# Third branch of a merged layer: projection multiplied chunk by chunk into four banks, gates after it

## The chip, the cores and the metric

One core of one Trainium2 chip runs one program. The metric is the device time of one execution in microseconds, as the median of several runs. Everything is float32; products are made of two fp32r parts per operand (below).

## The reference, cut to what matters

The program computes two model blocks on 256 tokens (held as two tiles of 128) of width 1024. The change lies in the first block. Its layer has three branches, whose outputs are projected, gated and summed, and then goes through an output projection and a mixture of 32 experts:

```python
merged = (jax.nn.sigmoid(ga) * (o_a @ w_branch_a)      # o_a: 256 x 1024
          + jax.nn.sigmoid(gb) * (o_b @ w_branch_b)    # o_b: 256 x 1024
          + jax.nn.sigmoid(gc) * (o_c @ w_branch_c))   # o_c: 256 x 2048, the third branch
x = x + gt1 * (merged @ w_out)
h2 = rmsnorm(x, norm2_g) * (1.0 + sc2) + sh2
x = x + gt2 * hier_moe(h2, rg_w, rg_b, re_w, re_b, e_gate, e_up, e_down)
```

`ga`, `gb` and `gc` are columns of `h @ w_in`. Each expert has three matrices of 1024 x 512, so the experts' weights are 32 x 3 x 2 MB = 192 MB, and all of them are read.

## The kernel before, in words

Every engine runs its own list of instructions in order, and they meet only in semaphores. Weights come in loads of 1 MB, issued by SyncE (`fetch`) into a ring of five places named "raw". A load is cut into pieces of 128x1024 elements, two per load. ScalarE copies a piece to a rounded high part H (line 1597), VectorE subtracts it to get the low part L (line 2304), and TensorE multiplies with both: `three` (lines 651 to 653) issues high x high, high x low and low x high. There are four places for H and L, so ScalarE and VectorE run up to three pieces ahead of the one in use (`reach`, `ahead`), and a piece's H waits until TensorE has used the piece four before it. Where an engine's list has an evaluation between two pieces, it stands behind the H or L of up to three pieces further on.

A piece of `gemm2` is 24 matmuls of 128x256. The branch stages run `for i in range(4)`: two pieces of the gate `{name}g{i}` into one bank, then the projection `{name}w{i}`. For the third branch (name "C") the projection has depth 2048, so it takes four pieces and two banks. ScalarE makes the sigmoid of the gate, VectorE multiplies it with the projection (line 2560), GpSimd adds the product to the merged sum `mg` (line 3351). In the third branch these two work on halves of 256 columns. TensorE takes banks 0 to 3 in turn for its products (`take("m", ...)`) and banks 4 to 7 for side work (`take("s", ...)`); a `take` waits until the reader of the bank's former content has finished (`taken`). Counted from the start of the program, the second branch's last projection, Bw3, has the 64th turn counted from zero and so lies in bank 0; the third branch's first gate takes bank 1.

After the third branch's last gate, `mg` is split for the output projection: `mg_high(j)` on ScalarE (line 1820) and `mg_low(j)` on VectorE (line 2580) take quarter j. Quarters 0 to 2 are split beside the last projection, quarter 3 behind it. `w_out` then runs pieces of 12 matmuls of 128x512. Its first two pieces (depths 0 to 3, quarters 0 and 1) are multiplied as they come. The third and fourth (depths 4 to 7, quarters 2 and 3) are held, and TensorE waits for the L of the fourth before it uses either. The pieces of this stage are called wo0, wo1, wo2 and wo3 here. ScalarE issues the H of wo3 after `mg_high(3)`, and VectorE its L after `mg_low(3)`.

Behind `w_out` come the routing and the experts, in eight groups. Free memory holds expert weights early: places "ex" (in part the former place of the second branch's operand) and "pre" (in part that of the third branch's operand `ocT`, whose high part lies at 35360 to 39456 and low part at 39456 to 43552). SyncE fetches ex 9 in the second branch, ex 0 to 4 with the first two quarters of the third, ex 10, pre 4 and pre 1 around the last, pre 0 and pre 2 once the last projection is done, four more "ex" after pieces of `w_out`, and pre 5, 6 and 3 once the router's logits are there. The raw ring's places go to expert weights as the last pieces before the experts are used. All later expert loads wait until an earlier group has used their place.

Of the kernel before, what the change touches and what calls it, by code (L numbers as in the profile page):

```python
# [140 lines left out]
def build(nc, a, out, scr):  # L141
    with ExitStack() as ctx:
# [254 lines left out]
        plan_branch("C", GC, a["w_branch_c"][0], 16, [])  # L397
# [83 lines left out]
        gs = {"A": mem(37152, 512), "B": mem(44064, 512), "C": mem(43552, 512)}  # L481
# [98 lines left out]
        adas = {"A": later[4:8], "B": later[12:16], "C": []}  # L580
# [39 lines left out]
        def tensor(e, w):  # L620
# [336 lines left out]
            def branch(name, XT, ready, kc):  # L957
                for i in range(4):
                    if name == "C" and i == 2:
                        router_bias()  # L960
                    gemm2(f"{name}g{i}", hT, h_ready)
                    gemm2(f"{name}w{i}", XT, ready, kc)
                    if name != "C":
                        ada(*adas[name][i])
                    elif i < 2:
                        ada_sum(10 + i)

# [553 lines left out]
            branch("C", ocT, lambda k: ("ocT", k // 2), 16)  # L1521
# [47 lines left out]
        def scalar(e, w):  # L1569
# [226 lines left out]
            def branch(name):  # L1796
                for i in range(4):
                    def ev_gate(p):
# [5 lines left out]
                        elif name == "C":  # L1804
                            w.wait_ge("full", ("ada", 5))
                        taken(e.activation(gs[name], b[:, :], ACT.Sigmoid), p.name, p.g, also=[("bg_s", name, i)])
                    run(f"{name}g{i}", ev_gate)
                    if name == "C" and i == 3:
                        e.activation(eps[:, 2:3], eps[:, 0:1], ACT.Sqrt)
                        for j in range(3):  # L1810
                            mg_high(j)
                    run(f"{name}w{i}")
                    if name != "C":
# [359 lines left out]
            branch("C")  # L2173
            mg_high(3)
# [93 lines left out]
        def vector(e, w):  # L2268
# [276 lines left out]
            def branch(name):  # L2545
                for i in range(4):
                    def ev_out(p):
                        n = 256 if name == "C" else 512
                        b = got(p.name, 0, p.b) if name == "C" else got(p.name, 0)
                        key = (p.name, 0, p.b) if name == "C" else (p.name, 0)  # L2550
                        o = 256 * p.b if name == "C" else 0
                        s = gs[name][:, o:o + n]
                        w.wait_ge("bg_s", name, i)
                        if name == "A":
                            w.wait_ge("ob2")
                            taken(e.tensor_tensor(mg[:, 512 * i:512 * i + 512], s, b[:, :], ALU.mult), *key,
                                  also=[("bs", "A", i), ("mg", "A", i)])
                        else:
                            c = o if name == "C" else 0
# [1094 lines left out]
```

## Time and profile before

| | us |
| --- | --- |
| median of 3 runs (2052.53 to 2053.99) | 2053.32 |
| the profiled execution | 2053.77 |
| its span | 2051.9 |
| TensorE busy | 1908.7 (93%) |
| VectorE busy | 1133.1 (55%) |
| ScalarE busy | 903.5 (44%) |
| GpSimd busy | 118.8 (6%) |

The span is what the profiler records of the program; the execution's own time is 1.87 us longer. In the page's 40 slices of 51.3 us the DMA engines move 150 to 290 GB/s up to the eleventh slice, 354 in the twelfth, and 410 to 426 in the thirteenth to twentieth, where TensorE's busy share falls to six to eight tenths. A busy TensorE is not TensorE at its peak, since the ends of matmuls are modelled. In a timeline, a row with a count merges neighbours, and its duration reaches from the first one's start to the last one's end.

### The profile page before, as it was taken

The numbers are of one execution on the slowest core, as the hardware profiler recorded it, in microseconds if no ns is written. First come the engines' busy times: TensorE is split into PE (matmuls) and PEld (weight loads), VectorE is DVE, ScalarE is ACT, GpSimd is POOL, SyncE is SP. The second block draws the span as 40 slices with busy tenths as digits, with TensorE's granted clock in tenths as the row PEclk, the third lists the DMA queues.
The fourth block names the chain that finished last, engine by engine and source line by source line (L and its number), as shares of the span: only waits on it lengthen the run. The fifth ranks groups of instructions, "written<-read, shape, count | busy, mean of one in ns | idle before, by whom it ended". The sixth has DMA issues, their size and how long they took to land.

```text
span 2051.9 us, 30543 instructions
## 1 busy us (share of the span) xinstructions
PE 1908.7 (93%) x12777; PEld 1485.8 (72%) x12777; DVE 1133.1 (55%) x1523; ACT 903.5 (44%) x1289; POOL 118.8 (6%) x101
## 2 busy tenths in 40 slices
PE   9999999999999866766699999999999999999998
PEld 7899988889984211111178888888888888988887
DVE  3678876678542110101156666756667666756666
ACT  4655555544342100000045555545456554675544
POOL 0244331001000000000000000000000000000000
PEclk9999999999999988788899999999999999999999
DMA  9654546788899999999985755545554555525552
GB/s 349 211 159 153 164 145 226 231 269 283 288 354 410 424 426 425 426 425 424 421 290 192 243 190 184 166 164 175 192 188 163 186 190 192 174 85 172 188 185 83
DMA packets 241761, 503.51 MB, mean 245 GB/s; under 512 B 11457, under 2 KB 165714, under 8 KB 222418
## 3 DMA queue, kind: packets, MB, share of 16 engines
q1 hardware_dynamic: 240720, 500.70, 67.8%
q8 instruction: 103, 1.69, 0.3%
q10 hardware_dynamic: 898, 0.80, 0.1%
q14 instruction: 40, 0.33, 0.0%
HBM read 500.07 MB, written 1.07 MB: 244 GB/s over the span
## 4 chain that ended last, share of the span: by engine, by line
PE 73%; DMA 14%; DVE 7%; ACT 3%; issue 2%; SPq 1%; POOL 0%; ACTq 0%; DVEq 0%
PE bank L651 14%; PE bank L712 14%; PE bank L653 13%; PE bank L652 13%; PE bank L714 7%; DMA m<-in_expert_w_up 4%; DMA m<-in_expert_w_down 4%; DMA m<-in_expert_w_gate 4%; PE bank L1115 3%; DVE m L2304 2%; PE bank L1126 2%; ACT m L1597 1%; PE bank L996 1%; SPq L3414 1%; DMA m<-in_ffn_w_in 0%
## 5 line engine op out<-in xcount | busy, mean ns | idle before, releaser
L2304 DVE TENSOR_TENSOR m<-m,m 128x1024 fp32r<-128x1024 f32 x505 | 625.7, 1254 | 287.0 <-ACT m L1597 284.8
L651 PE MATMUL bank<-m,m 128*128 128x256 f32 (+1 forms) x1960 | 658.4, 336 | 6.6 <-DVE m L2304 3.0
L653 PE MATMUL bank<-m,m 128*128 128x256 f32 (+1 forms) x1960 | 645.6, 329 | 0.0
L652 PE MATMUL bank<-m,m 128*128 128x256 f32 (+1 forms) x1960 | 645.2, 329 | 0.0
L1597 ACT ACTIVATE m<-m 128x1024 fp32r<-128x1024 f32 x505 | 524.2, 1054 | 223.1 <-PE bank L653 203.9
L712 PE MATMUL bank<-m,m 128*128 128x512 f32 x1248 | 439.8, 394 | 0.0
L651 PEld LDWEIGHTS bank<-m,m 128*128 128x128 f32 x1960 | 368.6, 188 | 55.7 <-DVE m L2304 10.0
L653 PEld LDWEIGHTS bank<-m,m 128*128 128x128 f32 x1960 | 368.6, 188 | 36.5
L652 PEld LDWEIGHTS bank<-m,m 128*128 128x128 f32 x1960 | 368.9, 188 | 33.8 <-issue 1.2
L714 PE MATMUL bank<-m,m 128*128 128x256 f32 x1248 | 352.7, 283 | 0.0
L712 PEld LDWEIGHTS bank<-m,m 128*128 128x128 f32 x1248 | 234.4, 188 | 54.0
L714 PEld LDWEIGHTS bank<-m,m 128*128 128x128 f32 x1248 | 234.6, 188 | 1.6
L1115 PE MATMUL bank<-m,m 128*32 128x512 f32 x1024 | 163.7, 674 | 59.8 <-DMA m<-in_expert_w_gate 33.3
L1115 PEld LDWEIGHTS bank<-m,m 128*32 128x32 f32 x1024 | 39.7, 121 | 175.3 <-issue 85.6
L1948 ACT ACTIVATE m<-bank 128x256 f32<-128x256 f32 x156 | 59.2, 379 | 161.5 <-PE bank L714 161.5
L1126 PE MATMUL bank<-m,m 128*32 128x512 f32 x512 | 91.3, 679 | 36.6 <-DMA m<-in_expert_w_down 30.8
L2855 DVE TENSOR_TENSOR m<-bank,m 128x256 f32<-128x256 f32 x156 | 65.6, 422 | 59.6 <-ACT m L1948 54.9
L1126 PEld LDWEIGHTS bank<-m,m 128*32 128x32 f32 x512 | 19.2, 122 | 101.1 <-DMA m<-in_expert_w_down 56.5
L2730 DVE TENSOR_TENSOR m<-bank,m 128x512 f32<-128x512 f32 x16 | 10.3, 686 | 142.1 <-PE bank L1126 142.1
L2724 DVE SCALAR_TENSOR_TENSOR m<-bank,m,m 128x512 f32<-128x512 f32 x8 | 6.0, 750 | 118.3 <-PE bank L1115 118.3
L2751 DVE TENSOR_TENSOR m<-m,bank 128x512 f32<-128x512 f32 x32 | 21.3, 686 | 87.1 <-PE bank L1198 87.1
L1859 ACT ACTIVATE m<-bank 128x512 f32<-128x512 f32 x8 | 4.8, 597 | 133.0 <-PE bank L1115 133.0
(352 smaller groups left out, 1384.1 us busy)
## 6 DMA issues: line engine op xcount, KB each, us to landing
m<-in_ffn_w_in SPq DMA_DIRECT2D x88, 1024.0 KB, 5.1
m<-in_w_in SPq DMA_DIRECT2D x60, 1024.0 KB, 5.2
m<-in_ffn_w_out SPq DMA_DIRECT2D x44, 1024.0 KB, 5.0
m<-in_expert_w_up SPq DMA_DIRECT2D x40, 1024.0 KB, 21.8
m<-in_expert_w_down SPq DMA_DIRECT2D x34, 1024.0 KB, 18.0
m<-in_expert_w_gate SPq DMA_DIRECT2D x33, 1024.0 KB, 22.8
m<-in_expert_w_gate SPq DMA_DIRECT2D x15, 2048.0 KB, 23.4
m<-in_expert_w_down SPq DMA_DIRECT2D x13, 2048.0 KB, 17.9
```

Of the source, the lines that this page charges most:

```text
L651: e.matmul(o, s[0], m[0], start=first, stop=False, skip_group_check=skip)
L652: e.matmul(o, s[0], m[1], start=False, stop=False, skip_group_check=skip)
L653: return e.matmul(o, s[1], m[0], start=False, stop=last, skip_group_check=skip)
L712: e.matmul(b[:, :].rearrange("p (h n) -> p h n", h=2), H, N.both[:, k], start=k == 0, stop=False, skip_group_check=True)
L714: ins = e.matmul(b[:, 0:256], L, N.T[0][:, k, :], start=False, stop=k == 7, skip_group_check=True)
L1115: ins = e.matmul(b[32 * j:32 * j + 32, :], XG(q, q + 1)[:, 0, k, 32 * j:32 * j + 32], block(ld, i), start=k == 0, stop=k == 7, skip_group_ ...
L1126: ins = e.matmul(b[n][32 * j:32 * j + 32, :], eT[q % 2][:, 128 * c + 32 * j:128 * c + 32 * j + 32], ld.raw[:, 1024 * i + 512 * n:1024 * i ...
L1597: inc(e.activation(rv(fit(q.H, q.view.shape)), q.view, ACT.Copy), "h", skey(q, "H"))
L1948: inc(e.activation(fb[6][:, 256 * b:256 * b + 256], k[:, 256:512], ACT.Copy), "ffn", (f"f{z}c", n, c, b))
L2304: inc(e.tensor_tensor(rv(fit(q.L, q.view.shape)), q.view, fit(q.H, q.view.shape), ALU.subtract), "l", skey(q, "L"))
L2751: taken(e.tensor_tensor(o, o if q else x[:, t, 512 * n:512 * n + 512], b[:, :], ALU.add), "ey", q, t, n, also=[("y", q, t, n)])
L2855: taken(e.tensor_tensor(o, k[:, 0:256], fb[6][:, 256 * b:256 * b + 256], ALU.add), f"f{n}{z}{c}", b, also=[(f"f{z}a", n, c, b)])
```

## The change

The third branch's projection is no longer four separate quarters. Its operand is multiplied in order of depth: a load holds four depth chunks of 128 by 512 output columns, cut into two pieces of 256 columns, and the four quarters' sums grow side by side in banks 0 to 3, one full bank each. Seven loads (14 pieces, list "Ca") run first, then the four gates Cg0 to Cg3 in the side banks, then the eighth load (list "Cz", two pieces), which ends quarters 2 and 3. VectorE's product and GpSimd's addition now take 512 columns at once. The number and size of the matmuls, of the loads, and of the H and L parts are as before. `mg_high` and `mg_low` of quarters 0 and 1 stand ahead of Cz, those of quarters 2 and 3 behind it. The first half of `ocT` (depths 0 to 7) is read for the last time by the eighth piece of Ca; SyncE then fetches pre 5 and pre 1 into its place. Pre 0 moves behind the router's logits, since the router's operand now lies there.

```diff
@@ -273,6 +273,20 @@
+        def plan_third(gcol, W):
+            G["Ca"], G["Cz"] = [], []
+            for k0 in (0, 4, 8, 12):
+                for h in range(2):
+                    last = k0 == 12 and h == 1
+                    for i in range(4 if last else 0):
+                        plan_gemm2(f"Cg{i}", win, 8, [gcol + 256 * i])
+                    ld = load(lambda r: r.rearrange("p (k n) -> p k n", n=512),
+                              W[128 * k0:128 * k0 + 512, 512 * h:512 * h + 512].rearrange("(k p) n -> p k n", p=128))
+                    v = ld.raw.rearrange("p (k n) -> p k n", n=512)
+                    for i in range(2):
+                        G["Cz" if last else "Ca"].append(Piece(plan, ld, v[:, :, 256 * i:256 * i + 256], 1024, name="Cw",
+                                                               g=2 * h + i, k=k0, m=4, end=k0 == 12))
...
-        plan_branch("C", GC, a["w_branch_c"][0], 16, [])
+        plan_third(GC, a["w_branch_c"][0])
...
-        gs = {"A": mem(37152, 512), "B": mem(44064, 512), "C": mem(43552, 512)}
+        gs = {"A": mem(37152, 512), "B": mem(44064, 512), "C": [mem(43552, 512), mem(44064, 512)]}
...
-        wos = mem(36384, 512)
-        rj = mem(36896, 512)
-        rF = [v256(mem(o, 1024)) for o in (35360, 44576)]
+        wos = mem(38432, 512)
+        rj = mem(38944, 512)
+        rF = [v256(mem(o, 1024)) for o in (37408, 44576)]
...
+            def products(name):
+
+                for p in walk(name):
+                    w.wait_ge(*skey(p, "L"))
+                    o = take(p.g, "Cw", p.g) if p.k == 0 else bank[p.g]
+                    for b in range(2):
+                        for i in range(4):
+                            k = p.k + i
+                            w.wait_ge("ocT", k // 2)
+                            ins = three(o[:, 256 * b:256 * b + 256], parts(p, 256 * i + 128 * b, 128),
+                                        (ocT[0][:, k, :], ocT[1][:, k, :]), k == 0 and b == 0, k == 15, True)
+                    used(ins, p, *([("Cw", p.g)] if p.end else []))
+
+            def third_branch():
+                products("Ca")
+                for i in range(4):
+                    if i == 1:
+                        router_bias()
+                    gemm2(f"Cg{i}", hT, h_ready, at="s")
+                    if i < 2:
                         ada_sum(10 + i)
+                products("Cz")
+                turn["m"] = 0
...
@@ -1801,21 +1834,34 @@
...
+            def third_branch():
+                run("Ca")
+                for i in range(4):
+                    def ev_gate(p):
+                        b = got(p.name, p.g)
+                        if i >= 2:
+                            w.wait_ge("bs", "C", i - 2)
+                        elif i:
+                            w.wait_ge("bs", "B", 3)
+                        else:
+                            w.wait_ge("full", ("ada", 5))
+                        taken(e.activation(gs["C"][i % 2], b[:, :], ACT.Sigmoid), p.name, p.g, also=[("bg_s", "C", i)])
+                    run(f"Cg{i}", ev_gate)
+                e.activation(eps[:, 2:3], eps[:, 0:1], ACT.Sqrt)
+                mg_high(0)
+                mg_high(1)
+                run("Cz")
+                mg_high(2)
+                mg_high(3)
 
             def mg_high(j):
                 w.wait_ge(*skey(G["Cg3"][-1], "used"))
-                w.wait_ge("mg", "C", j, 1)
+                w.wait_ge("mg", "C", j, 0)
...
@@ -2545,33 +2590,41 @@
...
+            def third_branch():
+                def ev_out(i):
+                    b = got("Cw", i)
+                    s = gs["C"][i % 2]
+                    w.wait_ge("bg_s", "C", i)
+                    taken(e.tensor_tensor(s, s, b[:, :], ALU.mult), "Cw", i, also=[("bsv", "C", i)])
+                for n, p in enumerate(walk("Ca")):
+                    if n == 4:
                         router_weights()
+                for i in range(4):
+                    run(f"Cg{i}")
+                    if i < 2:
+                        ev_out(i)
                         ada_out(10 + i)
+                    if i == 1:
                         b = got("rbias")
                         taken(e.tensor_tensor(rt["bias"], b[:, 0:36], rB, ALU.add), "rbias")
+                mg_low(0)
+                mg_low(1)
+                run("Cz", lambda p: ev_out(p.g))
+                mg_low(2)
+                mg_low(3)
...
@@ -3343,16 +3395,11 @@
...
-                    def ev_out(p):
-                        o, n, b = (256 * p.b, 256, p.b) if name == "C" else (0, 512, 0)
-                        m = mg[:, 512 * i + o:512 * i + o + n]
-                        w.wait_ge("bsv", name, i, b)
-                        w.wait_ge(*(("mg", "A", 3) if name == "B" else ("mg", "B", 3, 0)))
-                        inc(e.tensor_tensor(m, m, gs[name][:, o:o + n], ALU.add), "mg", ("mg", name, i, b), ("bs", name, i))
-                    run(f"{name}g{i}")
-                    run(f"{name}w{i}", ev_out if name != "A" else None)
-                    if name != "C":
-                        run(("ada", *adas[name][i]))
+                    m = mg[:, 512 * i:512 * i + 512]
+                    w.wait_ge("bsv", name, i)
+                    w.wait_ge(*(("mg", "A", 3) if name == "B" else ("mg", "B", 3, 0)))
+                    s = gs["B"] if name == "B" else gs["C"][i % 2]
+                    inc(e.tensor_tensor(m, m, s, ALU.add), "mg", ("mg", name, i, 0), ("bs", name, i))
...
@@ -3432,18 +3479,8 @@
...
-                    if name == "C" and i == 3:
-                        w.wait_ge("taken", ("rbias",))
-                        fetch(first("ex", 10))
-                        w.wait_ge(*skey(G["Cg3"][-1], "used"))
-                        fetch(first("pre", 4))
-                        for p in G["Cw3"][:3]:
-                            ahead(p)
-                        w.wait_ge(*skey(G["Cw3"][1], "used"))
-                        fetch(first("pre", 1))
...
+            def third_branch():
+                for n, p in enumerate(G["Ca"]):
+                    ahead(p)
+                    if n == 2:
                         w.wait_ge("full", ("ocT", 7))
                         w.wait_ge(*skey(G["Bw3"][-1], "used"))
-                        for slot in ((0, 1), (2, 3))[i]:
+                        w.wait_ge("taken", ("cd", 3))
+                        for slot in (0, 1):
                             fetch(first("ex", slot))
-                        if i == 0:
-                            w.wait_ge("taken", ("cd", 3))
-                            fetch(first("ex", 4))
+                    if n == 5:
+                        for slot in (2, 3):
+                            fetch(first("ex", slot))
+                    if n == 8:
+                        fetch(first("ex", 4))
+                    if n == 10:
+                        w.wait_ge(*skey(G["Ca"][7], "used"))
+                        for slot in (5, 1):
+                            fetch(first("pre", slot))
+                run("Cg0", "Cg1")
+                w.wait_ge("taken", ("rbias",))
+                fetch(first("ex", 10))
+                run("Cg2", "Cg3")
+                w.wait_ge(*skey(G["Cg3"][-1], "used"))
+                fetch(first("pre", 4))
+                run("Cz")
...
-            w.wait_ge(*skey(G["Cw3"][-1], "used"))
-            for i in (0, 2):
-                fetch(first("pre", i))
+            w.wait_ge(*skey(G["Cz"][-1], "used"))
+            fetch(first("pre", 2))
...
-            for i in (5, 6, 3):
+            for i in (6, 0, 3):
```

## Rows read from the trace of the kernel before

**Rows 1.** Windows of the stretches: start:end, length, busy us (count) per engine, PEclk, DMA share, GB/s.

```profile
507.73:578.69 70.96, 70.96 (x646) 69.68 (x645) 39.68 (x46) 30.35 (x33) 7.35 (x8) 1.00 0.82 293
...
620.00:1050.00 430.00, 312.18 (x1874) 97.15 (x1865) 57.85 (x94) 34.40 (x61) 0.00 (x0) 0.86 1.01 421
```

**Rows 2.** What TensorE waited for, 440 to 1060 us: total us, times, longest.

```profile
PE bank L1115 <- DMA m<-in_expert_w_gate: 33.3, 15, 3.9
PE bank L1126 <- DMA m<-in_expert_w_down: 30.8, 18, 3.9
...
PE bank L651 <- DVE m L2304: 0.2, 1, 0.2
```

**Rows 3.** Timeline of TensorE: start, us, engine, line, operands [idle before <- releaser].

```profile
674.57 3.63 PE L1126 MATMUL bank<-m,m 128*32 128x512 f32 x28 [1.45 <-DMA m<-in_expert_w_down]
...
1030.96 3.62 PE L1126 MATMUL bank<-m,m 128*32 128x512 f32 x26 [0.20 <-DMA m<-in_expert_w_down]
```

**Rows 4.** Windows of 2 and 10 us around the end of the output projection.

```profile
582.00:584.00 2.00, 2.00 (x10) 1.65 (x9) 2.00 (x2) 0.80 (x1) 0.00 (x0) 1.00 0.33 115
584.00:594.00 10.00, 10.00 (x44) 8.10 (x43) 5.38 (x8) 3.99 (x6) 0.00 (x0) 1.00 0.99 394
594.00:596.00 2.00, 2.00 (x13) 1.66 (x12) 1.02 (x1) 0.64 (x2) 0.00 (x0) 1.00 0.31 123
```

**Rows 5.** Timeline of SyncE's DMA queue.

```profile
576.05 11.08 SPq L3414 DMA_DIRECT2D m<-in_expert_w_up  x5
595.04 7.82 SPq L3414 DMA_DIRECT2D m<-in_expert_w_down  x5
605.92 0.33 SPq L3414 DMA_DIRECT2D m<-in_expert_w_gate  x1
```

**Rows 6.** Timeline of TensorE at the stage's two ends.

```profile
507.73 0.28 PE L651 MATMUL bank<-m,m 128*128 128x256 f32 x1
...
567.30 0.28 PE L651 MATMUL bank<-m,m 128*128 128x256 f32 x1
...
578.70 0.39 PE L651 MATMUL bank<-m,m 128*128 128x512 f32 x1
...
584.27 0.39 PE L651 MATMUL bank<-m,m 128*128 128x512 f32 x1
...
603.54 0.66 PE L1015 MATMUL bank<-m,m 128*128 128x128 f32 x4 [0.37 <-DVE m L3159]
```

**Rows 7.** Timeline of VectorE.

```profile
485.15 0.69 DVE L2560 TENSOR_TENSOR m<-m,bank 128x512 f32<-128x512 f32 x1
485.75 3.44 DVE L2304 TENSOR_TENSOR m<-m,m 128x1024 fp32r<-128x1024 f32 x2
492.42 2.36 DVE L2304 TENSOR_TENSOR m<-m,m 128x1024 fp32r<-128x1024 f32 x2 [0.47 <-ACT m L1597]
507.93 0.69 DVE L2560 TENSOR_TENSOR m<-m,bank 128x512 f32<-128x512 f32 x1 [1.75 <-PE bank L653]
570.17 1.90 DVE L2580 TENSOR_TENSOR m<-m,m 128x512 fp32r<-128x512 f32 x3 [3.14 <-ACT m L1820]
580.83 0.69 DVE L2580 TENSOR_TENSOR m<-m,m 128x512 fp32r<-128x512 f32 x1 [1.51 <-ACT m L1820]
581.78 2.36 DVE L2304 TENSOR_TENSOR m<-m,m 128x1024 fp32r<-128x1024 f32 x2 [0.26 <-ACT m L1597]
```

**Rows 8.** Timeline of ScalarE.

```profile
569.52 1.66 ACT L1820 ACTIVATE m<-m 128x512 fp32r<-128x512 f32 x3
571.08 3.17 ACT L1597 ACTIVATE m<-m 128x1024 fp32r<-128x1024 f32 x3
580.16 0.63 ACT L1820 ACTIVATE m<-m 128x512 fp32r<-128x512 f32 x1 [2.99 <-POOL m L3351]
```

**Rows 9.** Timeline of GpSimd.

```profile
472.32 1.30 POOL L3351 TENSOR_TENSOR m<-m,m 128x512 f32<-128x512 f32 x1 [120.73 <-DVE m L2560]
485.91 2.20 POOL L3351 TENSOR_TENSOR m<-m,m 128x512 f32<-128x512 f32 x1 [12.29 <-DVE m L2560]
```

More of the change, by code:

```diff
@@ L579, in build @@
         rt["pr"] = tmp(64).rearrange("p (t e g) -> p t g e", t=2, g=4)
-        adas = {"A": later[4:8], "B": later[12:16], "C": []}
+        adas = {"A": later[4:8], "B": later[12:16]}
         def reach(p):
@@ L1520, in tensor @@
             ticks.join()
-            branch("C", ocT, lambda k: ("ocT", k // 2), 16)
+            third_branch()
             w_out()
@@ L1803, in ev_gate @@
                             w.wait_ge("oaL", 1)
-                        elif name == "C":
-                            w.wait_ge("full", ("ada", 5))
                         taken(e.activation(gs[name], b[:, :], ACT.Sigmoid), p.name, p.g, also=[("bg_s", name, i)])
                     run(f"{name}g{i}", ev_gate)
-                    if name == "C" and i == 3:
-                        e.activation(eps[:, 2:3], eps[:, 0:1], ACT.Sqrt)
-                        for j in range(3):
-                            mg_high(j)
                     run(f"{name}w{i}")
-                    if name != "C":
-                        run(("ada", *adas[name][i]))
+                    run(("ada", *adas[name][i]))
+            def third_branch():
[17 more added lines that the diff above has]
+                mg_high(3)
             def mg_high(j):
                 w.wait_ge(*skey(G["Cg3"][-1], "used"))
-                w.wait_ge("mg", "C", j, 1)
+                w.wait_ge("mg", "C", j, 0)
                 o = slice(512 * j, 512 * j + 512)
@@ L2172, in scalar @@
             ticks.join()
-            branch("C")
-            mg_high(3)
+            third_branch()
             def x_copy(g, t):
@@ L2547, in ev_out @@
                     def ev_out(p):
[L2548 to L2552, printed above, removed]
+                        b = got(p.name, 0)
+                        s = gs[name]
                         w.wait_ge("bg_s", name, i)
@@ L2555, in ev_out @@
                             w.wait_ge("ob2")
[L2556 removed]
+                            taken(e.tensor_tensor(mg[:, 512 * i:512 * i + 512], s, b[:, :], ALU.mult), p.name, 0,
                                   also=[("bs", "A", i), ("mg", "A", i)])
                         else:
[L2559 to L2570 removed]
+                            taken(e.tensor_tensor(s, s, b[:, :], ALU.mult), p.name, 0, also=[("bsv", name, i)])
+                    run(f"{name}g{i}")
+                    run(f"{name}w{i}", ev_out)
+                    run_ada(*adas[name][i])
+            def third_branch():
[6 more added lines that the diff above has]
+                    if n == 4:
+                        router_weights()
+                for i in range(4):
+                    run(f"Cg{i}")
+                    if i < 2:
+                        ev_out(i)
                         ada_out(10 + i)
[L2572 removed]
+                    if i == 1:
                         b = got("rbias")
                         taken(e.tensor_tensor(rt["bias"], b[:, 0:36], rB, ALU.add), "rbias")
+                mg_low(0)
[3 more added lines that the diff above has]
+                mg_low(3)
             def mg_low(j):
@@ L3147, in vector @@
             ticks.join()
-            branch("C")
-            mg_low(3)
+            third_branch()
             def ev_wo(p):
@@ L3434, in branch @@
                     run(f"{name}g{i}")
[L3435 to L3443 removed]
                     run(f"{name}w{i}")
[L3445 to L3446 removed]
+                    run(("ada", *adas[name][i]))
                     if name == "A" and i == 1:
```

24 lines of the change are left out of this document (2 added, 22 removed).

## The prediction

> **What bounds the kernel now.** The page's 40 slices come first: they show which stages are bound by what. From the thirteenth slice to the twentieth DMA moves up to 426 GB/s while TensorE is busy six to eight tenths. The windows put numbers to it [rows 1]: from 620 to 1050 us the DMA share is 1.01 at 421 GB/s, and TensorE is busy 312 of 430 us. The waits of TensorE from 440 to 1060 us name the cause: expert weights [rows 2]. TensorE first waits for such a load at 674 us, and last at 1030.96 us, when the last expert weights have come in [rows 3]. So the expert stage ends when its bytes are in. Before it the opposite holds. In the third branch (507.73 to 578.69 us) TensorE is busy 70.96 of 70.96 us at full clock, and DMA runs at a share of 0.82 [rows 1].
>
> A transfer made earlier shortens the whole only if it leaves fewer bytes for the stretch in which DMA never rests. That stretch starts late. In the 2 us from 582 DMA is busy 0.33, from 594 again 0.31, and between them 0.99 [rows 4]. A backlog can't leave such a gap, so by about 595 us everything issued up to then had landed. The next loads leave at 595.04 us in a group of five and at 605.92 us [rows 5]. These are the ones that wait for the last output-projection pieces and for the router's logits, which are TensorE's progress. As a check: by 595 us 15 of the 192 expert loads of 1 MB had been issued (the group of 595.04 not counted). The other 177 are 185.6 million bytes, and at 425 GB/s, the page's value for those slices, they take 436.7 us: 595 + 437 = 1032, against 1030.96 read [rows 3]. The end of the expert stage is thus TensorE's arrival at the end of the output projection, plus a fixed number of bytes.
>
> **The early transfers: 0 us.** Before, pre 1, pre 0 and pre 2 leave in and about the group at 576.05 us [rows 5]; after, pre 5 and pre 1 leave when the eighth piece of Ca is used, at about 540 us. But pre 0 moves from there to the place that pre 5 had, behind the logits. Before the gap at 594 us lie 15 loads either way, and behind it 177. Two loads are earlier in a stretch that already ends with an idle DMA. I take 0. The bounds: 0, and 2 loads x 1.05 MB / 0.425 = 4.9 us gained, if the gap is not what I read in it. That pre 0 is now late costs nothing by the same count: it has pre 5's position among the loads from 605.92 us, and it is first needed in the experts' third block, later than pre 5 was (the second block).
>
> **Matmuls, H and L, gates: 0 us.** 24 pieces of 24 matmuls stand on both sides. The pace is that of the stage, 2.85 us a piece: from 567.30 us (last gate done) to 578.70 us (first matmul of the output projection) are four pieces [rows 6]. TensorE waited 0.2 us in all for a low part [rows 2], so nothing can be won inside the stage. VectorE saves four products of the half width, and it was busy only 39.68 of 70.96 us [rows 1]. If a strided source (256 of 512 columns) made H or L slower, that cover of 31 us would hide it.
>
> **First new wait: 0.95 us.** Ca's first piece must use bank 0, and bank 0 holds Bw3. TensorE has the next matmul ready at 507.73 us; VectorE's product of Bw3 runs from 507.93 for 0.69 us [rows 6, 7], and the bank is free at 508.62. Such a release reaches TensorE in some 0.06 us: line 1015 starts at 603.54 after a VectorE product that ends at 603.48. So the stall is 508.68 - 507.73 = 0.95 us. Before, the next bank was bank 1, long free. Behind this wait on TensorE stands the whole stage. ScalarE and VectorE have three pieces ready and don't wait for it. Bounds: 0.8 us (the product alone, begun at once) and 1.2 us (weight load exposed again).
>
> **Second new wait: 1.5 us.** Let T be the time at which Cg3 is multiplied (567.30 before). Before, four pieces follow until the output projection, now two: it can start at T + 5.70 (2 x 2.85). wo0 and wo1 take 584.27 - 578.70 = 5.57 us, so wo3's L must be there at T + 11.27 [rows 6]. Before, its L started 3.08 us after the last product matmul (581.78 - 578.70) and took 1.2 us, so it was there 1.3 us early [rows 7]. Now, step by step:
> - `mg_high` of quarters 0 and 1 starts at T + 2.22 (569.52), and the first H behind it at T + 3.26 (two copies of 0.52 us instead of three). That is wo1's H, ready at T + 4.3; the H of wo2 is ready at T + 5.3 [rows 8].
> - VectorE does `mg_low` 0 and 1 from T + 2.87 (570.17), wo1's L from T + 4.34, then quarter 2's product from T + 5.48 and wo2's L from T + 6.08 [rows 7].
> - GpSimd's addition of quarter 2 starts 0.76 us after its product does (485.15 to 485.91), at T + 6.25. It meets wo2's L, as in the second branch. There GpSimd takes 2.20 us instead of 1.30, and two L take 3.44 us instead of 2.36 [rows 7, 9]. The times fit taking turns: L from 485.75 to 486.98, the addition to 488.11, the next L to 489.19. So quarter 2 is added at T + 8.45.
> - Quarter 3's product (one operand in a bank) ran beside GpSimd unharmed, as at 472.32. It ends at T + 7.9, but its addition comes behind quarter 2's: T + 8.55 to 9.85 at 1.30 us. Meanwhile `mg_high(2)` ends at T + 9.15, and `mg_low(2)` waits its turn behind the addition, until T + 10.5.
> - `mg_high(3)` starts at T + 9.9. From there the row pattern of before holds: H of wo3 0.54 us later (580.16 to 580.70), and L 1.08 us after that (581.78), 1.2 us long [rows 7, 8]. wo3 is ready at T + 12.75.
> The stall is 12.75 - 11.27 = 1.5 us. Bounds: with no contention at all the chain is 0.9 us shorter (0.6 us); with quarter 3's addition also at 2.20 us it is 0.9 us longer (2.4 us).
> The Trainium skill, "SBUF — State Buffer", section "Who interferes with whom", says that VectorE and GpSimd share one port pair, which an operation holds for its full length while the other blocks. By that rule it is 1.5 us, since only the first addition finds VectorE ahead of it. By a reading in which both run slowed whenever they overlap, it is about 2.4 us. The starts and ends above fit the rule.
>
> What is late next: nothing. wo4 needs wo0's place, free long before.
>
> **Sum.** Both waits lie before the loads of 595 us and so pass in full to the end: 0.95 + 1.5 = 2.5 us. The profiled execution took 2053.77 us, 0.45 above the median, so I expect 2056.3 against it, and 2055.8 against the median of 2053.32. Bounds of the sum: 1.4 to 3.6 us, so 2054.7 to 2056.9. A difference under 0.2% (4.1 us) can't be told here from no change; the forecast lies within it.
>
> **Rivals.**
> - A, early bytes count. If DMA still had work queued through the gap, 2 MB less remain behind it: 4.9 us. With both waits 2050.9, and 2048.4 if the waits are hidden too. For it: the stage behind is bound by DMA and by nothing else. Against it: shares of 0.33 and 0.31 within 12 us [rows 4], and the count to 1032 us.
> - B, slower: the tail of the merged sum. Place: between Cg3 and wo3, with only two pieces as cover. ScalarE's list is in order, so wo3's H stands behind `mg_high(3)`, which stands behind two full-width additions on GpSimd. If VectorE's L of wo2 or `mg_low(2)` gets in before quarter 3's addition, that takes 2.20 us too, and the L of wo3 then falls on a delayed VectorE at 2.3 us instead of 1.2: 0.9 + 1.1 more, a stall of 3.5 us, 4.5 in all, 2057.8 or somewhat more. It decides once wo3's L is ready after T + 14.4 (a stall over 3.1). For it: three of four full-width additions of the second branch took 2.20 us. Against it: each of them started just behind an L, and quarter 3's need not.
> - C, the change doesn't show: quarter 3 makes it in time, and only the bank's wait is left, at 2054.3.
>
> **How the numbers follow.** The forecast has 0.60, A 0.14, B 0.18, C 0.08. I predict 2055.8. Slower by over 0.2% (above 2057.4) is B and a little of the forecast's upper end: 0.20. Faster by over 0.2% (below 2049.2) is A's better half: 0.10. The same is left with 0.70. The likeliest case alone gives 2054.7 to 2056.9. For 8 in 10 the range takes in most of B and A's 2050.9: 2050.9 to 2058.4.
>
> **What would show it.** TensorE idle about 0.95 us at its first matmul of the stage, released by the product of line 2560's successor. A second idle stretch of 1.5 us some 5.6 us after the output projection begins, released by an L, with GpSimd's additions at 2.20 and 1.30 us ahead of it. A gap of DMA before the last pieces of the output projection, as now or wider. The first wait of TensorE for expert weights, the last one and everything behind them later by the sum of the two. The prediction is wrong if DMA has no gap there, if the last wait for expert weights ends earlier than 1031 us, or if TensorE idles elsewhere in the stage.

## The result

| | before | changed |
| --- | --- | --- |
| median, us | 2052.68 (20 runs) | 2056.07 (20 runs) |
| range, us | 2051.39 to 2053.99 | 2053.62 to 2057.49 |
| profiled execution, us | 2053.77 | 2056.46 |
| its span, us | 2051.9 | 2054.6 |

The changed kernel takes 1.0014 times as long, with a 95% interval of 1.0008 to 1.0020: 3.4 us by the medians (1.6 to 4.1 us by the interval). It is slower, by less than the 0.2% named in the prediction; but a difference of this size can be told from no change here, since the interval excludes it. The forecast was 2.5 us more, at 2055.8 us. That the time itself lies within 0.3 us of the forecast is partly luck: 2055.8 was counted from the 2053.32 us of three runs, 0.6 us above the 2052.68 us of these twenty. The difference, 3.4 us against 2.5 with bounds of 1.4 to 3.6, is the fairer comparison.

The views of the changed kernel stand in the order of the prediction's steps. First, what TensorE waited for between 440 and 1060 us; lines 665 to 667 are the three products that were 651 to 653.

```profile
PE bank L1148 <- DMA m<-in_expert_w_gate: 32.8, 15, 3.8
PE bank L1159 <- DMA m<-in_expert_w_down: 32.1, 16, 3.9
PE bank L1148 <- DMA m<-in_expert_w_up: 25.0, 13, 4.4
...
PE bank L665 <- DVE m L2349: 1.4, 2, 1.2
PE bank L665 <- DVE m L2601: 0.9, 1, 0.9
```

Two waits are new against [rows 2], of 0.87 and 1.24 us where 0.95 and 1.5 us were forecast. The timeline of TensorE says where they lie: at the stage's first matmul, and at wo3.

```profile
508.71 0.36 PE L665 MATMUL bank<-m,m 128*128 128x256 f32 x1 [0.87 <-DVE m L2601]
...
580.28 0.39 PE L665 MATMUL bank<-m,m 128*128 128x512 f32 x1
...
587.25 0.47 PE L665 MATMUL bank<-m,m 128*128 128x512 f32 x1 [1.24 <-DVE m L2349]
...
606.61 0.66 PE L1048 MATMUL bank<-m,m 128*128 128x128 f32 x4 [0.37 <-DVE m L3211]
...
1033.68 3.62 PE L1159 MATMUL bank<-m,m 128*32 128x512 f32 x26 [0.17 <-DMA m<-in_expert_w_down]
```

The end of the output projection has its mark in the transposes that wait for VectorE: 606.61 us, against 603.54 in [rows 6]. That is 3.07 us later. The last wait for expert weights ends 2.72 us later (1033.68 against 1030.96 in [rows 3]), and the span is 2.7 us longer. So what was lost before the experts came out at the end nearly whole. To compare runs more finely I measure from the start of VectorE's last product of the second branch (507.87 here, 507.93 in [rows 7]). From it to the transposes are 98.74 us here and 95.61 before: 3.13 us more.

### The profile page after: what moved, and what is told of

Read it like the earlier page. It is cut to its first block, busy times and chain, and to the rows that moved or that the text cites. A ratio compares the mean times of both kernels' runs of the same rounds, so it can differ in the third digit from the quotient of the medians.

```text
span 2054.6 us, 30540 instructions
## 1 busy us (share of the span) xinstructions
PE 1907.1 (93%) x12777; PEld 1487.1 (72%) x12777; DVE 1134.2 (55%) x1519; ACT 903.2 (44%) x1289; POOL 119.0 (6%) x97
## 4 chain that ended last, share of the span: by engine, by line
PE 73%; DMA 14%; DVE 6%; ACT 3%; issue 2%; SPq 1%; POOL 0%; ACTq 0%; DVEq 0%
PE bank L665 14%; PE bank L726 13%; PE bank L667 13%; PE bank L666 13%; PE bank L728 7%; DMA m<-in_expert_w_up 5%; DMA m<-in_expert_w_gate 4%; DMA m<-in_expert_w_down 4%; PE bank L1148 3%; PE bank L1159 2%; DVE m L2349 2%; SPq L3461 1%; ACT m L1630 1%; PE bank L1029 1%; DMA m<-in_ffn_w_in 0%
```

## The second wait, step by step

VectorE (line 2349 makes low parts, 2611 the branch's product, 2633 `mg_low`), ScalarE (1853 the gate, 1866 `mg_high`, 1630 high parts) and GpSimd (3402, the addition), each in its own timeline:

```profile
507.87 0.69 DVE L2601 TENSOR_TENSOR m<-m,bank 128x512 f32<-128x512 f32 x1 [1.76 <-PE bank L667]
...
578.91 1.23 DVE L2349 TENSOR_TENSOR m<-m,m 128x1024 fp32r<-128x1024 f32 x1 [0.17 <-ACT m L1630]
580.06 0.68 DVE L2611 TENSOR_TENSOR m<-m,bank 128x512 f32<-128x512 f32 x1
580.65 1.22 DVE L2349 TENSOR_TENSOR m<-m,m 128x1024 fp32r<-128x1024 f32 x1
581.79 0.68 DVE L2611 TENSOR_TENSOR m<-m,bank 128x512 f32<-128x512 f32 x1
583.72 1.11 DVE L2633 TENSOR_TENSOR m<-m,m 128x512 fp32r<-128x512 f32 x1 [1.25 <-ACT m L1866]
584.98 0.69 DVE L2633 TENSOR_TENSOR m<-m,m 128x512 fp32r<-128x512 f32 x1
585.93 3.50 DVE L2349 TENSOR_TENSOR m<-m,m 128x1024 fp32r<-128x1024 f32 x3 [0.26 <-ACT m L1630]
```

```profile
574.78 0.60 ACT L1853 ACTIVATE m<-bank 128x512 f32<-128x512 f32 x1 [1.73 <-PE bank L667]
...
576.80 1.14 ACT L1866 ACTIVATE m<-m 128x512 fp32r<-128x512 f32 x2
577.84 1.99 ACT L1630 ACTIVATE m<-m 128x1024 fp32r<-128x1024 f32 x2
583.05 0.63 ACT L1866 ACTIVATE m<-m 128x512 fp32r<-128x512 f32 x1 [3.22 <-POOL m L3402]
584.31 0.63 ACT L1866 ACTIVATE m<-m 128x512 fp32r<-128x512 f32 x1 [0.63 <-POOL m L3402]
584.85 2.94 ACT L1630 ACTIVATE m<-m 128x1024 fp32r<-128x1024 f32 x3
```

```profile
580.82 3.46 POOL L3402 TENSOR_TENSOR m<-m,m 128x512 f32<-128x512 f32 x2 [15.62 <-DVE m L2611]
...
580.82 2.20 POOL L3402 TENSOR_TENSOR m<-m,m 128x512 f32<-128x512 f32 x1 [15.62 <-DVE m L2611]
```

T, the end of the last gate's matmuls, is 574.58 us here (the gate's sigmoid starts 0.20 us behind it, as 567.50 did behind 567.30). The first addition runs from T + 6.24 for 2.20 us beside a low part. The second starts at 582.99 us and takes 1.29 us, until 584.28 us. Quarter 3's product from a bank runs during the first and isn't longer for it (0.68 us). `mg_low(2)` takes 1.11 instead of 0.69 us, since it starts while the second addition still runs. `mg_high(3)` starts at T + 9.73, and wo3's low part, the first third of the merged row from 585.93 us, takes 1.23 us and is done at T + 12.6. The prediction had T + 6.25, 2.20 and 1.30, T + 9.9 and T + 12.75. TensorE idled 1.24 us, where 1.5 was forecast; its next matmul started 1.40 us later than its pace has it (587.25 - 580.28 - 5.57).

This is the exclusive turn-taking for which the prediction named the Trainium skill, "SBUF — State Buffer", section "Who interferes with whom". The trace agrees with it: whichever started first kept its length (1.29 us for the second addition), and the other's row was longer. The reading in which every overlap slows both would have made the stall 2.4 us.

## The experiments

Each edit is against the changed kernel, and each time stands beside runs of the kernel before on the same chip. Differences between two changed kernels are differences of their distances (medians) to those runs. "Arrival" is the distance from VectorE's product to the transposes, as above: 95.61 before, 98.74 changed.

**Other banks.**

```diff
-                    o = take(p.g, "Cw", p.g) if p.k == 0 else bank[p.g]
+                    o = take((p.g + 1) % 4, "Cw", p.g) if p.k == 0 else bank[(p.g + 1) % 4]
...
                 products("Cz")
-                turn["m"] = 0
+                turn["m"] = 1
```

> The changed kernel with quarter g of the projection in bank (g + 1) mod 4 instead of bank g, and the output projection's turn starting at bank 1. My theory: TensorE's idle stretch of 0.87 us at the stage's first matmul goes, since bank 1 has long been free; the second one (1.24 us, at wo3) stays; the transposes that end the output projection come 0.9 to 1.0 us earlier than in the changed kernel (606.61 us there), and the last wait for expert weights (1033.68 us) and the whole run by as much: 2.1 us above the kernel before instead of 3.1. Rival 1 (the wait is for something else than the bank, such as the operand or the low part): the idle stretch stays at 0.87 us. Rival 2 (the end of the expert stage does not follow TensorE's arrival): the stretch goes but the last wait for weights stays at 1033.7 us.

Measured: 2055.2 us against 2052.49, ratio 1.0012 (1.0003 to 1.0021), 2.7 us above before, where 2.1 was expected. TensorE no longer waits at the stage's start. In its timeline only the second wait is left, and the transposes come earlier:

```profile
585.51 0.47 PE L665 MATMUL bank<-m,m 128*128 128x512 f32 x1 [1.23 <-DVE m L2349]
...
604.87 0.66 PE L1048 MATMUL bank<-m,m 128*128 128x128 f32 x4 [0.37 <-DVE m L3211]
```

The arrival is 97.11 us (604.87 - 507.76), 1.63 us less than in the changed kernel. That is more than the expected 0.9 to 1.0: 0.51 us is the matmul pace (below), and 0.17 us the delay and the slow first matmul that come with a stop. The span is 1.7 us shorter than the changed kernel's (2052.9 against 2054.6 us), so the end followed the arrival. The bank was the cause of the first wait.

**wo3's parts first.**

```diff
                 run("Cz")
+                ahead_to(G["wo"][3].j + 1)
                 mg_high(2)
...
                 run("Cz", lambda p: ev_out(p.g))
+                ahead_to(G["wo"][3].j + 1)
                 mg_low(2)
```

> The changed kernel with the high part of wo3 issued on ScalarE ahead of mg_high(2), and its low part on VectorE ahead of mg_low(2). My theory: wo3's parts were late only because of their place in two in-order lists behind GpSimd's additions. They are ready 3 us before they are needed, the quarters 2 and 3 of the merged sum come just in time (quarter 3 is needed 1.4 us later than wo3's low part), and the idle stretch of 1.24 us goes or shrinks under 0.3 us; the run is 1.2 to 1.5 us shorter than the changed kernel. Rival (the two full-width additions themselves bound the start): TensorE still idles 1 us or more, now released by mg_low, and nothing is gained.

Measured: 2055.07 us against 2052.49, ratio 1.0012 (1.0003 to 1.0022). That is 0.8 us less than the changed kernel by the medians, where 1.2 to 1.5 were expected. The second wait's idle row is gone, although both additions now take over 2.2 us each. GpSimd, VectorE and TensorE of this kernel (3404 the addition, 2350 low parts, 2635 `mg_low`):

```profile
579.30 4.44 POOL L3404 TENSOR_TENSOR m<-m,m 128x512 f32<-128x512 f32 x2 [15.61 <-DVE m L2612]
```

```profile
580.87 1.72 DVE L2350 TENSOR_TENSOR m<-m,m 128x1024 fp32r<-128x1024 f32 x1
582.51 2.62 DVE L2635 TENSOR_TENSOR m<-m,m 128x512 fp32r<-128x512 f32 x2
```

```profile
584.10 0.40 PE L667 MATMUL bank<-m,m 128*128 128x512 f32 x1
584.44 0.47 PE L665 MATMUL bank<-m,m 128*128 128x512 f32 x1
```

wo3's low part is done at 582.6 us, and TensorE doesn't wait for it. It waits a little for `mg_low(2)`, which is longer for the second addition (1.78 us from 582.51, so until 584.29): the matmul at 584.44 us follows its neighbour by 0.34 us instead of 0.23. The stall of 1.40 us has shrunk to 0.11. The arrival is 96.93 us, 1.81 us less than in the changed kernel: these 1.29 us, and 0.51 us of matmul pace (below). So the additions by themselves hold up the output projection by 0.1 us only. The rest came from the place of wo3's parts behind them, in two in-order lists.

**Both edits together.**

> Both edits: quarters in banks 1, 2, 3, 0, and wo3's parts ahead of the last two quarters' splits. My theory: both idle stretches go; what stays over the kernel before is TensorE's slower pace in the projection (2.88 instead of 2.85 us a piece, 16 pieces, 0.5 us). The end of the output projection lies 0.5 to 0.7 us behind the kernel before (603.54 us), the run 0.5 to 0.8 us above it (ratio 1.0002 to 1.0004). Rival A (early bytes count): with the waits gone the run is 2.5 to 4.9 us below the kernel before (ratio 0.9976 to 0.9988).

Measured: 2053.24 us against 2052.49, ratio 1.0004 (0.9995 to 1.0013), which is 0.75 us above before. TensorE has no idle row between 500 us and the transposes:

```profile
603.58 0.65 PE L1048 MATMUL bank<-m,m 128*128 128x128 f32 x4 [0.37 <-DVE m L3213]
```

The arrival is 95.82 us, 0.2 above before, by the same short wait for `mg_low(2)` and the slow matmul behind it. The slower pace that was expected to stay, 0.5 us, isn't there. With the two waits went 2.6 of the 3.4 us (each alone took 0.7 and 0.8 us off by the medians, less than its row; the spread of the runs is of that size, and the arrivals part them better). The early transfers, now with nothing in their way, won nothing: rival A expected a ratio of 0.9988 at most, which lies outside the interval.

**The two transfers late again.** In place of the fetch of pre 5 and pre 1 after Ca's eighth piece:

```diff
             w.wait_ge(*skey(G["Cz"][-1], "used"))
-            fetch(first("pre", 2))
+            for i in (5, 1, 2):
+                fetch(first("pre", i))
```

> The changed kernel with pre 5 and pre 1 fetched only after the last piece of the projection, with pre 2, so none of the two transfers is early. My theory: the 15 loads still land before DMA's idle stretch at about 597 us, so the time is that of the changed kernel within 0.4 us (ratio to the kernel before 1.0012 to 1.0016), and DMA is still nearly idle for over 1 us before the group of five loads at 598 us. Rival A (early bytes count): two loads more remain behind, 4.9 us longer (ratio about 1.0038).

Measured: 2056.33 us against 2052.49, ratio 1.0017 (1.0008 to 1.0026). That is 3.8 us above before, against 3.4 of the changed kernel: the same within the runs' spread, and not 4.9 us more. One part of the expectation failed. DMA ran without a gap here from 588 to 604 us, where the changed kernel has one. Windows of 2 us of this kernel:

```profile
592.00:594.00 2.00, 2.00 (x11) 1.59 (x10) 1.97 (x3) 1.06 (x1) 0.00 (x0) 1.00 1.03 434
594.00:596.00 2.00, 2.00 (x10) 1.64 (x9) 1.86 (x4) 0.79 (x3) 0.00 (x0) 1.00 0.99 418
596.00:598.00 2.00, 2.00 (x12) 1.63 (x12) 1.03 (x1) 0.66 (x2) 0.00 (x0) 1.00 1.03 434
...
618.00:620.00 2.00, 2.00 (x20) 1.75 (x23) 1.03 (x5) 0.17 (x1) 0.00 (x0) 1.00 1.01 414
620.00:622.00 2.00, 2.00 (x24) 0.63 (x20) 0.23 (x2) 1.97 (x4) 0.00 (x0) 1.00 1.00 393
```

So a gap near 597 us isn't needed for the transfers to be worthless; the backlog was worked off later. Nor does DMA run short near 620 us here, as it does in the changed kernel, whose windows stand below: there DMA loses some 3.2 us between 596 and 600 us and 1.3 us near 620. The two late loads, 4.9 us of DMA time at 425 GB/s, filled both stretches and left an estimated 0.4 us over. That led to the next runs.

**One load more behind the logits, and two.**

```diff
             w.wait_ge(*skey(G["Cz"][-1], "used"))
-            fetch(first("pre", 2))
...
-            for i in (6, 0, 3):
+            for i in (6, 0, 2, 3):
```

> The changed kernel with pre 2 fetched behind the router's logits, after pre 0, instead of after the projection: 14 loads before DMA's idle stretch, 178 behind it. My theory: each load that crosses that stretch costs 1.05 MB / 0.425 = 2.5 us of the DMA-bound stage, so the last wait for expert weights ends near 1036.2 us and the run is 2.3 to 2.6 us longer than the changed kernel (ratio to the kernel before 1.0025 to 1.0028). Rival (the stage has slack in its order, or pre 2 is issued into a stretch with room): under 0.5 us.

Measured: 2057.51 us against 2053.23, ratio 1.0024 (1.0013 to 1.0034). That is 4.3 us above before and so 0.9 us above the changed kernel, where 2.5 was expected. The two intervals (1.6 to 4.1 and 2.7 to 7.0 us above before) overlap, so the times alone don't exclude 2.5. The windows give a reason for the smaller value. First the changed kernel around its two short stretches (columns as in [rows 1]), then this one:

```profile
596.00:598.00 2.00, 2.00 (x10) 1.63 (x9) 1.97 (x3) 0.91 (x4) 0.00 (x0) 1.00 0.19 78
598.00:600.00 2.00, 2.00 (x14) 1.75 (x13) 0.09 (x1) 0.87 (x2) 0.00 (x0) 1.00 0.54 86
...
620.00:622.00 2.00, 2.00 (x20) 1.02 (x22) 1.20 (x6) 1.15 (x3) 0.00 (x0) 1.00 0.78 270
622.00:624.00 2.00, 2.00 (x24) 0.65 (x20) 0.67 (x5) 1.97 (x4) 0.00 (x0) 1.00 0.99 348
```

```profile
594.00:596.00 2.00, 2.00 (x11) 1.61 (x10) 1.83 (x4) 0.72 (x2) 0.00 (x0) 1.00 0.02 8
596.00:598.00 2.00, 2.00 (x10) 1.60 (x9) 1.64 (x2) 0.72 (x2) 0.00 (x0) 1.00 0.00 0
...
620.00:622.00 2.00, 2.00 (x20) 0.71 (x22) 0.77 (x5) 1.59 (x3) 0.00 (x0) 1.00 1.02 426
622.00:624.00 2.00, 2.00 (x24) 0.65 (x20) 1.04 (x7) 1.97 (x4) 0.00 (x0) 1.00 1.01 422
```

The changed kernel runs short twice: before the group at 598.12 us, and again near 621 us. The second time all the loads issued up to 610 us are in, and the next places come free with the experts' first block. Its DMA queue shows both (the two issues at 608.99 us are the halves of one load, so eight loads leave from 598 to 610 us):

```profile
540.54 0.50 SPq L3461 DMA_DIRECT2D m<-in_expert_w_gate  x1
541.09 0.43 SPq L3461 DMA_DIRECT2D m<-in_expert_w_up  x1
...
598.12 7.83 SPq L3461 DMA_DIRECT2D m<-in_expert_w_down  x5
608.99 0.84 SPq L3459 DMA_DIRECT2D m<-in_expert_w_gate  x2
609.88 1.01 SPq L3461 DMA_DIRECT2D m<-in_expert_w_up  x2
618.87 0.33 SPq L3461 DMA_DIRECT2D m<-in_expert_w_down  x1
```

The second short stretch loses some 1.3 us of DMA time (270, 348 and 369 GB/s in three windows of 2 us, against 424). A ninth load among those of 598 to 610 us fills it, and only the remainder of its 2.5 us is paid. If so, a tenth must cost its full price. The next run tests that:

```diff
                 w.wait_ge(*skey(G["Cg3"][-1], "used"))
-                fetch(first("pre", 4))
                 run("Cz")
...
             w.wait_ge(*skey(G["Cz"][-1], "used"))
-            fetch(first("pre", 2))
...
-            for i in (6, 0, 3):
+            for i in (6, 4, 0, 2, 3):
```

> The changed kernel with two loads, pre 4 and pre 2, fetched behind the router's logits: 13 loads before DMA's first idle stretch and 10 in the groups behind it. The run with one load moved cost about 0.9 us instead of 2.5, and DMA no longer ran short near 620 us, where the changed kernel loses about 1.3 us of its rate. My theory now: what counts is when the bytes issued before the experts' first release (619 us) have been moved. The first moved load half fills that second short stretch (cost 1.2 us), the next one costs its full 2.5 us: 3.5 to 4 us above the changed kernel in all, ratio to the kernel before 1.0031 to 1.0034, with no short stretch at 620 us. Rival (the first theory, each load 2.5 us): 5 us, ratio 1.0038. Rival (loads are cheap, 0.9 us each): 1.8 us, ratio 1.0023.

Measured: 2060.06 us against 2052.82, ratio 1.0034 (1.0021 to 1.0046). That is 7.2 us above before, 3.8 us above the changed kernel and 2.9 above the run with one load moved. DMA no longer runs short near 620 us (the window from 620 has 414 GB/s). The expected 3.5 to 4 us are met, and both rivals (5 and 1.8 us) miss the median. Both ratios, 1.0038 and 1.0023, lie inside the interval, however, so the account by the later short stretch rests on the windows of the three kernels and on medians, not on times clear of noise.

**The pace of the projection.** In the changed kernel 14 pieces of Ca run at 2.88 us each (high parts 2.81 and 2.95 us apart), not at 2.85, which costs some 0.5 us. Two kernels were to name the cause. The first exchanges the loops:

```diff
-                    for b in range(2):
-                        for i in range(4):
+                    for i in range(4):
+                        for b in range(2):
```

> The changed kernel with the projection's inner loops exchanged: depth outside, 128-column half inside. Weights are then read at consecutive steps of 128, and the halves of the bank alternate. If the pace of 2.88 us a piece comes from the weights' step of 256 elements between two depths, it falls to 2.85 us (two pieces 5.70 instead of 5.76). If it comes from anything else (the piece, the operand, the bank), it stays at 5.76, or rises if alternating halves costs something. I hold the step for likelier, 0.6.

The second changes the layout of the parts:

```diff
-                        G["Cz" if last else "Ca"].append(Piece(plan, ld, v[:, :, 256 * i:256 * i + 256], 1024, name="Cw",
+                        z = v[:, :, 256 * i:256 * i + 256].rearrange("p k (b n) -> p b k n", b=2)
+                        G["Cz" if last else "Ca"].append(Piece(plan, ld, z, 1024, name="Cw",
...
-                            ins = three(o[:, 256 * b:256 * b + 256], parts(p, 256 * i + 128 * b, 128),
+                            ins = three(o[:, 256 * b:256 * b + 256], parts(p, 512 * b + 128 * i, 128),
```

> The changed kernel with the high and low parts laid out half by half (source view with the half ahead of the depth), so that the loops stay as they are and the weights of consecutive matmuls lie 128 elements apart. If the step of the weights sets the pace, two pieces take 5.70 us instead of 5.76; if not, 5.76. ScalarE's and VectorE's conversions read 128 elements at a time instead of 256; I expect them unchanged at 1.06 and 1.23 us.

Measured from VectorE's product to ScalarE's table load behind the last gate: 67.00 us with the loops exchanged (2055.82 us in one run), 67.52 with the other layout (2054.72 in one run), 67.52 in the changed kernel. Read alone, the pair is mixed: the exchange brought the fast pace, the layout didn't. But the kernels with late transfers and with wo3 first, whose TensorE instructions in this stage are those of the changed kernel, show 67.01 both, and the ones with one and with two loads moved 67.52. So the slow pace isn't a property of the order of matmuls, nor of the step between the weights, which is 128 elements in both of these kernels. All seven of these have TensorE's stop at bank 0. The kernels without the stop have 65.90 to 66.02, that is 1.0 to 1.1 us less than 67.01, and never the slow pace. Each value is from one profiled execution, so it isn't known whether the pace goes with the kernel or with the execution. Whether the stop is what lets the slow pace in stays open too.

**A version with one load more ahead.** This kernel has both waits mended. The router's operand lies in the place of the gates, the output projection's product with its gate is written back to its bank, and pre 0 is fetched after the projection. The edit, with that of the two waits left out:

```diff
-        wos = mem(38432, 512)
-        rj = mem(38944, 512)
-        rF = [v256(mem(o, 1024)) for o in (37408, 44576)]
+        rF = [v256(mem(o, 1024)) for o in (43552, 44576)]
+        rj = rF[1][:, :, 128:256]
...
+                if g and t:
+                    w.wait_ge("rsq", 3)
...
-                    taken(e.tensor_tensor(wos, b[:, :], gt1[:, 512 * p.g:512 * p.g + 512], ALU.mult), "wo", p.g, t)
-                    w.wait_ge("taken", ("wo", p.g, t))
+                    then(e.tensor_tensor(b[:, :], b[:, :], gt1[:, 512 * p.g:512 * p.g + 512], ALU.mult))
...
-                    inc(e.tensor_tensor(o, o, wos, ALU.add), "x", ("x1", t, p.g))
+                    taken(e.tensor_tensor(o, o, b[:, :], ALU.add), "wo", p.g, t, also=[("x1", t, p.g)])
...
-            fetch(first("pre", 2))
+            for i in (0, 2):
+                fetch(first("pre", i))
...
-            for i in (6, 0, 3):
+            for i in (6, 3):
```

> Both mended waits, and one load more before DMA's idle stretch: the router's operand moves to the place of the third branch's gates, the squares' unused output to a part of the operand that is not yet written, and the output projection's product with its gate is written back to its bank instead of to memory, so that pre 0 can be fetched with pre 2 right after the projection. 16 loads before the idle stretch, 176 behind. My theory: 2.5 us less than the kernel with both waits mended, so 1.7 to 2.0 us below the kernel before (ratio 0.9990 to 0.9992), if the product in the bank costs nothing. Rival: writing back to the bank and reading it again lengthens the output projection's end (each of four products and additions by some 0.1 us, of which two are on the way), and the gain is 2.2 us. Rival A' (a load is worth nothing): no gain.

Measured: 2051.76 us against 2053.23, ratio 0.9994 (0.9985 to 1.0003), 1.5 us below before. The same without the two edits of the transfers, to part places from load:

> The kernel with both waits mended and with the new places (router's operand in the gates' place, the product with the gate written back to its bank), but with pre 0 still fetched behind the logits. It parts the gain of the 16-load kernel (2.2 us below the one with both waits mended) into places and load. If the load made it: this one is within 0.4 us of the kernel with both waits mended (ratio 1.0003 to 1.0005). If the product in the bank made it: 1.5 us or more below that. By the theory of the second short stretch the load is worth only about 0.6 us, since DMA runs dry at 614 us there for some 2.7 us instead of 0.8.

Measured: 2053.46 us against 2052.82, ratio 1.0002 (0.9993 to 1.0011), 0.6 us above before, as with both waits mended alone (0.75). So the new places cost and gain nothing that the runs show. And the 16-load kernel again beside it:

> The 16-load kernel once more, on the same chip and with the same runs of before as the one without the load. Theory of each load at 2.5 us: 2.5 us below it. Theory of the second short stretch: 0.6 us below it. The first measurement put it at 1.47 us below the kernel before.

Measured: 2052.26 us against 2052.82, ratio 0.9997 (0.9988 to 1.0006), 0.6 us below before. The load is worth 1.2 us here, and 2.2 us by the first measurement (-1.47 against 0.75). The second short stretch grows, as the windows of the first measurement show:

```profile
614.00:616.00 2.00, 2.00 (x20) 1.03 (x13) 0.00 (x0) 0.00 (x0) 0.00 (x0) 1.00 0.11 45
616.00:618.00 2.00, 2.00 (x23) 1.28 (x25) 1.26 (x6) 0.81 (x2) 0.00 (x0) 1.00 0.89 238
```

Both values lie between the two theories (0.6 and 2.5 us), and the spread of the runs doesn't part them. The traces of the second pair allow a better estimate than the 0.6: against 424 GB/s DMA loses about 1.1 us without the load (328, 332 and 373 GB/s in the windows from 618 to 624 us) and 2.7 us with it (295, 86 and 311 from 614 to 620), 1.6 us more, which leaves 0.9 us of the load's 2.5. Both intervals of this version include 1. It is the best of all that were run, but not shown to be faster than the kernel before.

## Why the prediction was right, point by point

- **What bounds the kernel.** Right: two waits of TensorE, taken out, took 2.6 of 3.4 us off the end.
- **The first wait.** Forecast 0.95 us. The idle row is 0.87 us, and the next matmul starts 1.04 us after the point at which it would have (508.71 against 507.67, which is 0.20 us before VectorE's product). The bank was the cause. The release took longer than reckoned: 0.15 us from the end of VectorE's row at 508.56 us, where I had taken 0.06 us from a transpose. And a matmul behind a stop is slow itself (0.36 instead of 0.28 us), so that the next follows 0.19 instead of 0.12 us later. The stop costs 1.11 us in all, within the bounds.
- **The second wait.** Forecast 1.5 us, idle row 1.24 us, the next matmul 1.40 us late. From there to the transposes are 19.36 us instead of 19.27, nearly all of it the slow matmul behind the stop. The chain was right step by step; `mg_high(3)` came 0.17 us earlier than reckoned.
- **The pace.** The term "Matmuls, H and L, gates: 0 us", at 2.85 us a piece, failed by 0.51 us (67.52 against 67.01). It was the one term at nothing that wasn't nothing, and in three of the seven traces with TensorE's stop it didn't appear. The sum 1.11 + 0.51 + 1.40 + 0.09 makes up 3.11 of the 3.13 us by which the arrival moved.
- **The early transfers at 0 us.** The value was right, the reason only in part. I took the gap at 594 us for the point up to which a transfer made earlier gains nothing. It isn't: with both transfers late DMA had no gap there, and the time was the same. What fits all the runs is the later short stretch, between the loads issued with the logits and the experts' first release of places. The count to 1032 us held, since between the two DMA rests hardly at all, and a count from either gives nearly the same end. By the first reason each load across the gap is worth 2.5 us; measured by the medians were 0.9 us for the first load taken back, 2.9 for the second, and 1.2 to 2.2 for one added. None of these is clear of the spread of the runs by itself; the 3.8 us of the first two together are (4.3 to 9.4 us above before, against 1.6 to 4.1).
- **Rivals.** A fell with the kernel in which nothing stood in the transfers' way. B's contention (both additions at 2.20 us or more) did appear in the kernels with wo3's parts first. There it cost 0.2 us at the matmuls that wait for `mg_low(2)`, because wo3's parts no longer stood behind it. C did not occur.

## What to carry to other kernels

Before moving transfers earlier into a stage bound by compute, look for the last place before the DMA-bound stretch at which DMA runs short: in this case bytes that are in by then were worth nothing, and bytes moved across it were worth their time less what the short stretch absorbs. When operands that were spread over a bank rotation are gathered in fixed banks, check which bank the previous stage used last. When the last pieces before a dependent product become fewer, check what stands ahead of the next operands in each in-order list, and put what can go first ahead of what must wait.

## What was not expected of the hardware

- The pace of one and the same matmul sequence was 2.85 us a piece in some traces and 2.88 in others, at a granted clock of 1.00 in both. The slow one came only where TensorE had stopped at the start of the sequence (in four of seven traces; in none of the five of changed kernels without the stop, nor in that of the kernel before).
- GpSimd's addition of 128x512 took 1.28 to 1.30 us alone or when it had started first, and 2.20 us when a VectorE operation with both operands in memory had. The waiting side's row includes its wait, on either engine: `mg_low(2)` shows 1.11 us for 0.69 us of work.
- A matmul of 128x256 started 0.15 us after the end of the VectorE row that released it (508.56 to 508.71 us), a transpose 0.06 us after its own (603.48 to 603.54 us).
